# The remainder of a weight piece written over the raw piece in its ring slot, with six rounded-part buffers and a split five pieces ahead of TensorE

## What is computed

```python
def swiglu(x, w1, w3, w2):
    return (jax.nn.silu(x @ w1) * (x @ w3)) @ w2
...
    top_v, top_i = lax.top_k(logits, TOP_K)
    gates = jax.nn.softmax(top_v, axis=-1)
...
    for e in range(N_EXPERTS):
        out = out + combine[:, e:e + 1].astype(t.dtype) * swiglu(t, w1[e], w3[e], w2[e])
...
        u = depthwise_conv_2(h @ w_up[l], up_conv_w[l], up_conv_b[l], 1, 1)
        gate, val = jnp.split(u, 2, axis=-1)
        x = x + (jax.nn.gelu(gate) * val) @ w_down[l]
```

## Time and profile before

| | us |
|---|---|
| median of 3 runs (2238.98 to 2248.5) | 2240.61 |
| time of the profiled execution | 2246.18 |
| span of its profile (first to last instruction) | 2244.4 |

### The profile page before, as it was taken

One profiled execution on the slowest core, in us unless ns is written; L12 is line 12 of the kernel. 1 busy time (PEld: TensorE's weight loads), 2 busy tenths in 40 slices (PEclk: granted clock), 3 DMA queues, 4 the chain that ended last, 5 costly groups with the idle time before them and its releaser, 6 DMA issues.

```text
span 2244.4 us, 26185 instructions
## 1 busy us (share of the span) xinstructions
PE 2170.1 (97%) x10706; PEld 1747.6 (78%) x10706; DVE 1525.1 (68%) x1803; ACT 1098.9 (49%) x1102; POOL 58.1 (3%) x64
## 2 busy tenths in 40 slices
PE   8999999999999999999999999999999999999998
PEld 7578588875785787878788787888778786758997
DVE  4665644466656787888888886544488888546666
ACT  1233243312331676767677674434367674444554
POOL 0120000001200000000000000000000000100000
PEclk9999999999998999999999999999999999999999
DMA  8202364522023798989999896555479896316460
GB/s 315 75 1 76 137 219 150 206 100 75 1 76 132 269 368 312 371 302 363 340 346 370 322 372 238 188 188 187 174 278 370 312 370 232 121 38 221 173 225 20
DMA packets 209150, 484.44 MB, mean 216 GB/s; under 512 B 9200, under 2 KB 15088, under 8 KB 208112
## 3 DMA queue, kind: packets, MB, share of 16 engines
q1 hardware_dynamic: 209008, 482.50, 59.3%
HBM read 481.44 MB, written 1.05 MB: 215 GB/s over the span
## 4 chain that ended last, share of the span: by engine, by line
PE 85%; DVE 9%; ACT 3%; issue 2%; POOL 1%; DMA 0%; DVEq 0%; ACTq 0%; SPq 0%; POOLq 0%
PE bank L966 20%; PE bank L968 20%; PE bank L967 20%; PE bank L594 12%; PE bank L795 5%; PE bank L601 2%; PE bank L756 1%; DVE b_arena L1359 1%; DVE b_X L1365 1%; DVE e_lo L1842 1%; ACT e_hi L2247 1%; PE bank L873 1%; DVE b_XT L1359 1%; PE bank L711 1%; DVE b_arena L1365 1%
## 5 line engine op out<-in xcount | busy, mean ns | idle before, releaser
L1842 DVE TENSOR_TENSOR e_lo<-b_ring,e_hi 128x2048 fp32r<-128x2048 f32 (+1 forms) x407 | 924.8, 2280 | 345.8 <-ACT e_hi L2247 343.3
L2247 ACT ACTIVATE e_hi<-b_ring 128x2048 fp32r<-128x2048 f32 (+1 forms) x407 | 776.5, 1911 | 315.0 <-PE bank L968 310.9
L966 PE MATMUL bank<-e_hi,e_xh 128*128 128x512 f32 (+1 forms) x1200 | 475.1, 396 | 21.6 <-issue 10.2
L968 PE MATMUL bank<-e_hi,e_xl 128*128 128x512 f32 (+1 forms) x1200 | 468.4, 390 | 0.0
L967 PE MATMUL bank<-e_lo,e_xh 128*128 128x512 f32 (+1 forms) x1200 | 468.3, 390 | 0.0
L966 PEld LDWEIGHTS bank<-e_hi,e_xh 128*128 128x128 f32 x1200 | 228.3, 190 | 70.0 <-issue 24.0
L966 PE MATMUL bank<-e_hi,e_th 128*128 128x512 f32 x688 | 269.2, 391 | 0.4 <-DVE e_tl L1846 0.4
L967 PE MATMUL bank<-e_lo,e_th 128*128 128x512 f32 x688 | 268.0, 389 | 0.0
L968 PE MATMUL bank<-e_hi,e_tl 128*128 128x512 f32 x688 | 267.7, 389 | 0.0
L968 PEld LDWEIGHTS bank<-e_hi,e_xl 128*128 128x128 f32 x1200 | 228.1, 190 | 47.8
L967 PEld LDWEIGHTS bank<-e_lo,e_xh 128*128 128x128 f32 x1200 | 228.7, 191 | 45.0
(11 more groups left out here) (235 smaller groups left out, 2214.6 us busy)
## 6 DMA issues: line engine op xcount, KB each, us to landing
b_ring<-in_moe_w SPq DMA_DIRECT2D x168, 2048.0 KB, 9.8
b_ring<-in_ffn_w SPq DMA_DIRECT2D x15, 2048.0 KB, 8.4
b_ring<-in_w_in SPq DMA_DIRECT2D x14, 2048.0 KB, 10.0
b_ring<-in_w_up SPq DMA_DIRECT2D x12, 2048.0 KB, 8.0
b_ring<-in_w_down SPq DMA_DIRECT2D x6, 2048.0 KB, 8.5
b_ring<-in_w_o SPq DMA_DIRECT2D x4, 2048.0 KB, 7.8
b_gain<-in_gains SPq DMA_DIRECT2D x6, 1024.0 KB, 4.8
b_ring<-in_w_out SPq DMA_DIRECT2D x2, 2048.0 KB, 7.8
```

The costliest lines, as they stand in the source:

```text
L966: e.matmul(out, ah, bh, start=first, stop=False)
L968: return e.matmul(out, al, bh, start=False, stop=last)
L1842: e.tensor_tensor(lo, raw, r32(hi), ALU.subtract).then_inc(lo_dve.sem)
L2247: return e.activation(out, x, ACT.Copy)
```

## The change

Four things are changed together.

1. `lo` has no buffers of its own any more. `rest` is a second name, of type fp32r, for the same SBUF as the ring, and DVE writes the remainder in place over the raw piece. (To place them at one address, several constant and state tensors are laid out in another order.)
2. A ring slot is therefore in use until PE has finished its last piece: the signal of every weight use of the three feed-forwards goes from `lo_dve(...)` to `piece(...)`.
3. The room goes to `hi`: `NH` from 3 to 6.
4. `LEAD = 5`: `splits_at(p, first, end)` says which pieces are split at step p. From the start of a feed-forward it takes two pieces a step until the split is five pieces ahead, and then one a step, piece p + 5. Over the eight experts it runs through without starting again.

No matmul, copy or subtraction is added or removed.

```diff
-NR, NH = 4, 3
+NR, NH, LEAD = 4, 6, 5
...
+        with ExitStack() as over:
+            ring = [over.enter_context(nc.sbuf_tensor(f"b_ring{i}", [128, SLOT], F32)) for i in range(NR)]
+        rest = [sb(f"rest{i}", [128, SLOT], F32R) for i in range(NR)]
...
-            split = [[eb(f"{n}{i}", [128, 2048], F32R) for n in ("hi", "lo")] for i in range(NH)]
-            e_hi, e_lo = ([b[j] for b in split] for j in range(2))
+            e_hi = [eb(f"hi{i}", [128, 2048], F32R) for i in range(NH)]
...
-                        use(rows8(w, 512 * u, widths[u]), lo_dve(last[k]))
+                        use(rows8(w, 512 * u, widths[u]), piece(last[k]))
...
+        def splits_at(p, first, end):
+
+            def upto(i):
+                return min(end, i + 1 + min(LEAD, 2 + i - first))
+
+            return range(upto(p - 1) if p > first else first + 2, upto(p))
...
-                        if p + 2 < ends:
-                            split_rest(p + 2)
+                        for i in splits_at(p, first, ends):
+                            split_rest(i)
...
-                        if p + 2 < ends:
-                            split_round(p + 2)
+                        for i in splits_at(p, first, ends):
+                            split_round(i)
...
-                    if i + 2 < len(last_ff):
-                        split_round(FF2_P + i + 2)
+                    for n in splits_at(FF2_P + i, FF2_P, FF2_P + len(last_ff)):
+                        split_round(n)
```

More of the change, by code:

```diff
@@ L283, in two_blocks @@
         bank = [ctx.enter_context(nc.psum_tensor(f"bank{i}", [128, 512], F32)) for i in range(8)]
-        cst = sb("cst", [128, CTOT])
-        cols, rows = sb("cols", [128, COLN]), sb("rows", [128, ROWN])
+        cols, stat, comb = sb("cols", [128, COLN]), sb("stat", [128, 2, 16]), sb("moe_comb", [128, 2, 8])
+        with ExitStack() as over:
+            ring = [over.enter_context(nc.sbuf_tensor(f"b_ring{i}", [128, SLOT], F32)) for i in range(NR)]
+        rest = [sb(f"rest{i}", [128, SLOT], F32R) for i in range(NR)]
         X, XT = sb("X", [128, 2, D]), sb("XT", [128, DC, 256])
         gain = sb("gain", [128, 2 * D])
-        ring = [sb(f"ring{i}", [128, SLOT]) for i in range(NR)]
-        stat, sc, newt = sb("stat", [128, 2, 16]), sb("sc", [128, 512]), sb("newt", [128, 2, 24])
+        cst, rows = sb("cst", [128, CTOT]), sb("rows", [128, ROWN])
+        sc, newt = sb("sc", [128, 512]), sb("newt", [128, 2, 24])
         ba, pw = sb("ba", [128, 8, 16]), sb("pw", [128, 2, 256])
-        comb, sel = sb("moe_comb", [128, 2, 8]), sb("moe_sel", [128, 2, 8])
+        sel = sb("moe_sel", [128, 2, 8])
         rank, flag = sb("rank", [128, 2, 8]), sb("flag", [128, 8], mybir.dt.int32)
@@ L497, in gated_uses @@
                     use(w2[512 * (u - 1):512 * (u - 1) + widths[u - 1], :].rearrange("(c p) n -> p c n", p=128),
-                        lo_dve(last[k]))
+                        piece(last[k]))
                     k += 1
@@ L535, in two_blocks @@
             n = FF2_AT + 3 * u
-            use(rows8(a["w_up_2"], 512 * u, 512), lo_dve(last_of[n]))
-            use(rows8(a["w_up_2"], FF2 + 512 * u, 512), lo_dve(last_of[n + 1]))
+            use(rows8(a["w_up_2"], 512 * u, 512), piece(last_of[n]))
+            use(rows8(a["w_up_2"], FF2 + 512 * u, 512), piece(last_of[n + 1]))
             use(a["w_down_2"][512 * u:512 * u + 512, :].rearrange("(c p) n -> p c n", p=128),
-                lo_dve(last_of[n + 2]))
+                piece(last_of[n + 2]))
         def slot(n, width=512):
@@ L549, in gated_pieces @@
             for u, h, size in pieces_of(widths):
-                pieces.append((ring_in(at + u), ring[(at + u) % NR][:, size * h:size * h + size], size))
+                raw, lo = (of[(at + u) % NR][:, size * h:size * h + size] for of in (ring, rest))
+                pieces.append((ring_in(at + u), raw, lo, size))
         gated_pieces(FF0_AT, FF0_UNITS)
@@ L555, in two_blocks @@
         for kind, k, n, q in last_ff:
-            r = ring[n % NR]
-            raw = r[:, 2048 * q:2048 * q + 2048] if kind == "d" else slot(n)[:, :, 256 * q:256 * q + 256]
-            pieces.append((ring_in(n), raw, 2048))
+            raw, lo = (of[n % NR][:, 2048 * q:2048 * q + 2048] if kind == "d" else view(of[n % NR][:, :], 8, 512)[:, :, 256 * q:256 * q + 256]
+                       for of in (ring, rest))
+            pieces.append((ring_in(n), raw, lo, 2048))
         def place(p):
@@ L564, in split_views @@
         def split_views(p):
-            _, raw, size = pieces[p]
-            hi, lo = e_hi[place(p)][:, 0:size], e_lo[place(p)][:, 0:size]
+            _, raw, lo, size = pieces[p]
+            hi = e_hi[place(p)][:, 0:size]
             if len(raw.shape) == 3:
-                return raw, hi.rearrange("p (c n) -> p c n", c=8), lo.rearrange("p (c n) -> p c n", c=8)
+                hi = hi.rearrange("p (c n) -> p c n", c=8)
             return raw, hi, lo
+        def splits_at(p, first, end):
+            def upto(i):
+                return min(end, i + 1 + min(LEAD, 2 + i - first))
+            return range(upto(p - 1) if p > first else first + 2, upto(p))
         att_order = []
@@ L971, in take_piece @@
                 e.wait_ge(*lo_dve(p))
-                return e_hi[place(p)], e_lo[place(p)]
+                return split_views(p)[1:]
             def gated(widths, at, unit, tiles, first=None, aside=None, where=(0, 1)):
@@ L1325, in last_feed @@
                         b = up.take()
-                        h3, l3 = view(hi[:, :], 8, 256), view(lo[:, :], 8, 256)
+                        h3, l3 = hi, lo
                         for f in range(2):
@@ L1846, in rest_of, with gated @@
                 e.tensor_tensor(lo, src, r32(hi), ALU.subtract).then_inc(out, n)
-            def gated(widths, at, unit, tiles, ends, aside=None):
+            def gated(widths, at, unit, tiles, first, ends, aside=None):
                 p, inc = at, 2 // tiles
@@ L2004, in aside @@
                         picks(ex + 1, 0, 2)
-                gated(FFE_UNITS, at, 6 + 7 * ex, tiles, at + 42 + 2 * more, aside)
+                gated(FFE_UNITS, at, 6 + 7 * ex, tiles, MOE_P, FF2_P, aside)
                 e.wait_ge(*piece(at + 41))
@@ L2186, in last_feed @@
                     q = k % 2
-                    if i + 2 < len(last_ff):
-                        split_rest(FF2_P + i + 2)
+                    for n in splits_at(FF2_P + i, FF2_P, FF2_P + len(last_ff)):
+                        split_rest(n)
                     if kind == "d":
@@ L2222, in dve @@
             turn_split(0)
-            gated(FF0_UNITS, FF0_P, 0, 2, MOE_P)
+            gated(FF0_UNITS, FF0_P, 0, 2, FF0_P, MOE_P)
             add_feed(ALPHA, piece(MOE_P - 1))
```

## The result

| | before | after |
|---|---|---|
| median us | 2242.09 (4 runs) | 2533.91 (4 runs, 2524.21 to 2544.83) |
| span of the profile | 2244.4 | 2522.4 |
| ratio | | 1.1299, 95% interval 1.1245 to 1.1352 |

The forecast was 2505 with a range of 2410 to 2590.

A forecast was written before the change was run, and what follows sets the result against it. The prediction took PE, busy 97% of the span, to bound the kernel. Profiled 2246.2 + 175 (expert stops) + 70 (clock) + 20 (last feed-forward) = 2511; the median lies 5.6 lower, 2505 us, range 2410 to 2590.

The forecast's parts named there:

- Direction and mechanism: One-block experts: slower, 0.92; a load lands in the activations' path, closing a loop of 20.6 to 20.7 us against 16.82.
- a stop elsewhere than before w3: Sign of being wrong: in one-block experts, PE's new idle of 3.9 us should stand before w3's first matmul, following `e_tl`.
- 152 to 162 forecast: Sign in the profile after: gathers stand 152 to 162 us apart.
- The stops in the experts, +175: Seven experts: first stop 4.8 us, the others 3.9, and 0.9 near the end, 25 us an expert, +175 in all.
- The landing, 7.7 and not 11.0: Load in the experts' loop: lands 7.7 us after issue, as with a short queue, not 11.0 as with a full one.
- Rival (b): Load queue stays full: landings take 9.8 to 11 us, each of 46 stops grows, up to 2600 or 2655; chance 0.07.
- The clock, +70 in all: PE at half clock after 8 in 9 of 46 stops, 42 in experts, 4 in the last stage, 1.7 us each: +70.
- Rival (a): The clock holds: same stops, but PE comes back at full speed, 2436 us; chance 0.10.
- The last feed-forward, +20 and 7 of clock: Last feed-forward: PE stops 4.7 us before `d`, four times, and a shorter one at the start, +20; clock counted separately.
- The unit: One-block expert, distance between two `e_th`: from 16.82 to 20.7 us at full clock, about 22.3 with the clock lost.
- The frame: Whole kernel: 2511 us in terms of the profiled execution, with the median of the runs 5.6 lower, 2505.
- Rival (d): Nothing that counts: ACT waits for landings but catches up, being idle 26% of the stretch, 2241 us; chance 0.04.

The follow-up runs named there:

- `warm`: The changed kernel with three more throwaway matmuls on PE ahead of each stop in a one-block expert: 2461.71 us, ratio 1.0991.

## Why the prediction was right, point by point

- **Direction and mechanism** held: a load in the path of the activations, the stop ahead of w3 behind `e_tl`, 35 times, ACT's wait naming the landing, the two-block stretches unchanged, stops ahead of `d` in the last feed-forward. One thing was not said: the first stop of each expert stands at the transposes of unit 0, behind `e_h`, and not before w3. Its length was forecast (4.8; seven waits of 4.6 to 5.4), its place was not, and a stop elsewhere than before w3 had been named as a sign of being wrong. The cause is the same one step earlier: in the fourth expert the product starts on DVE at 1238.56, at the end of a remainder whose `hi` had waited 5.27 us for a landing. The first six gathers stand 156.2, 163.2, 164.3, 162.9 and 163.7 us apart, four of five past the 152 to 162 forecast; the larger loss of clock (below) goes that way.
- **The stops in the experts, +175.** Measured 166 us as waits, a typical one 3.7 and not 3.9; 187 in the kernel whose stops were filled, which keeps some lost clock. The term was right to within 9 us on the waits.
- **The landing, 7.7 and not 11.0.** The load of the turn above took 7.8, and the 18 loads from 1068 to 1216 us took 7.4 to 9.5 with a median of 7.8. The thinning of the queue was right: DMA share 0.75 there. Rival (b), the queue stays full, fell by this.
- **The clock, +70 in all.** In the experts it is 251 - 166 = 85, by difference, where I had 42 x 1.7 x 8/9 = 63. This is the term that was too small, by 22; that the stops were put 9 too high hid part of it, which is luck. I took 3.4 us of half clock behind each stop as the common case, but in the experts after, the clock record has 26 stretches of 3.4 and 19 of 6.8, and the mean is 0.93 over two whole units. (Together they are 218 us at half clock against 27 before, 95 us of work more; a part of the stretches lies inside the stops, where it costs nothing.) The upper end of the range, called the double of this term, was 156, which is 2.2 times the 70. Rival (a), the clock holds, fell; it was tried by `warm`, whose 2462 is above (a)'s 2436: in its experts the whole cost is 187 against the 175 of the sum, and its last feed-forward, where nothing was filled, kept its own lost clock.
- **The last feed-forward, +20 and 7 of clock.** Measured +30: 21.7 us of stops in 5 waits, four of 4.3 to 5.7 and one of 1.9; the rest, 8, goes to the clock by difference.
- **The unit:** 22.3 was given with the clock lost, 22.36 is the median; the loop at full clock 20.7, measured 20.74.
- **The frame.** I subtracted 5.6 us because the median of before lay below its profiled execution. After, the profiled execution (2524.21) is the lowest of four, and the median lies 9.7 above it. In terms of the profiled execution the forecast was 2511 and the time 2524, a miss of 13; the other 16 of the 29 us by which the median was missed are this. The four executions (2524, 2532, 2536, 2545 us) had a mean granted clock of 0.943, 0.938, 0.935 and 0.933: where much of the time hangs on a clock that drops or doesn't, one execution says less about the median.
- **Rival (d)**, that ACT waits for landings but catches up, is true for a lead of two or three, and fell at four and five. In the prediction the release alone was rightly judged harmless for a split two ahead.

Not tried: LEAD 5 with the old, earlier release. It needs a place for the remainders outside the ring, which neither kernel has beside six rounded-part buffers, and it was not built. So how the loop divides between release and lead is shown only from the side of the lead.

## What to carry to other kernels

Running further ahead on an in-order engine is not free lookahead: each step ahead moves a wait for a later load in front of today's work. Before deepening a lead, write down what stands behind the prefetch step on its engine, follow it to the instruction that releases the buffer for that same load, and add up that loop; if it is longer than the unit, the engine that was hidden becomes the bound. And by the same sum, though no run here varied it alone at a deep lead: if a buffer's release moves from an early consumer to the last one, the lead that the ring can carry shrinks by what lies between the two.

## What was not expected of the hardware

A stop of 3.7 us that comes back every 22 us costs the clock each time: all 42 have a stretch of 3.4 or 6.8 us at half clock beside them. In the experts after, the granted clock averages 0.92 over 1400.6 us, against 0.99 over 1149.8 before.

```profile
732.00:1881.80 1149.80, 1126.30 (x5156) 932.06 (x5156) 882.78 (x557) 721.02 (x491) 0.00 (x0) 0.99 0.83 304
729.40:2130.00 1400.60, 1212.50 (x5156) 983.90 (x5156) 879.53 (x557) 706.77 (x491) 0.00 (x0) 0.92 0.69 250
```

The stops of 2.3 to 2.6 us at the ends of experts in the same trace had one in one case of five, and at LEAD 4 those of 0.7 to 1.7 us had none. And filling the stops of 3.7 us with useless matmuls made the kernel 72 us faster.
